# Two transformer blocks on one core: the group behind six norms multiplies x before it is normalised

## The reference, cut to what matters

```python
def rms_norm(x, w=None):                      # first block, final norm
    y = xf * lax.rsqrt(jnp.mean(jnp.square(xf), axis=-1, keepdims=True) + EPS)
...
    x = x + g1 * (mixed @ w_out[l])
    h2 = rms_norm(x) * (1.0 + sc2) + sh2
    x = x + g2 * (jnp.square(jax.nn.relu(h2 @ w_ff1[l])) @ w_ff2[l])
    return rms_norm(x, final_norm_w)

def layer_norm(x, g, b):                      # second block
    mu = jnp.mean(xf, axis=-1, keepdims=True)
    var = jnp.mean(jnp.square(xf - mu), axis=-1, keepdims=True)
    y = (xf - mu) * lax.rsqrt(var + LN_EPS)
    return (y * g.astype(jnp.float32) + b.astype(jnp.float32)).astype(x.dtype)

def swiglu(x, w_gu, w_down):
    g, u = jnp.split(x @ w_gu, 2, axis=-1)
    return (jax.nn.silu(g) * u) @ w_down
...
        x = layer_norm(DEEPNORM_ALPHA * x + 0.5 * swiglu(x, ffn_w_gu[i, 0], ffn_w_down[i, 0]), ln_g[i, 0], ln_b[i, 0])
        y = moba_attention(...) or pool_mixer(...)
        x = layer_norm(DEEPNORM_ALPHA * x + y, ln_g[i, 1], ln_b[i, 1])
        x = layer_norm(DEEPNORM_ALPHA * x + 0.5 * swiglu(x, ffn_w_gu[i, 1], ffn_w_down[i, 1]), ln_g[i, 2], ln_b[i, 2])
```

## Time and profile before

| what | value |
|---|---|
| time, median of 3 executions | 1534.44 us (1533.14 to 1536.07) |
| profiled execution, first to last instruction | 1538.2 us |
| TensorE busy | 1504.7 us (98%) |
| VectorE busy | 1085.1 us (71%) |
| ScalarE busy | 824.3 us (54%) |
| POOL busy | 184.3 us (12%) |
| mean granted TensorE clock | 0.996 |
| dummy products at the borders (L868) | 147, of 10345 TensorE products |

### The profile page before, as it was taken

One profiled execution on the slowest core, in us unless ns is written; L12 is line 12 of the kernel. 1 busy time (PEld: TensorE's weight loads), 2 busy tenths in 40 slices (PEclk: granted clock), 3 DMA queues, 4 the chain that ended last, 5 costly groups with the idle time before them and its releaser, 6 DMA issues.

```text
span 1538.2 us, 26135 instructions
## 1 busy us (share of the span) xinstructions
PE 1504.7 (98%) x10345; PEld 1389.6 (90%) x10345; DVE 1085.1 (71%) x1409; ACT 824.3 (54%) x1067; POOL 184.3 (12%) x169
## 2 busy tenths in 40 slices
PE   8999999999999999999999999999999999999997
PEld 7999998989988899888998988889988898988887
DVE  7788988787877656666576686665766659876655
ACT  5655567654555336555444555554655545565543
POOL 0120003562000010000130020001300013020001
PEclk9999999999999999999999999999999999999999
DMA  8957756645455754455544345555455553355550
GB/s 327 364 209 274 268 193 226 226 153 218 176 197 183 269 186 166 173 192 189 192 161 168 110 165 177 193 181 187 164 178 193 182 187 135 141 191 191 189 192 28
DMA packets 43397, 295.89 MB, mean 192 GB/s; under 512 B 5052, under 2 KB 7228, under 8 KB 8750
## 3 DMA queue, kind: packets, MB, share of 16 engines
q1 hardware_dynamic: 40574, 280.24, 50.2%
q0 software_dynamic: 2736, 14.41, 2.8%
HBM read 291.44 MB, written 3.19 MB: 192 GB/s over the span
## 4 chain that ended last, share of the span: by engine, by line
PE 59%; DVE 5%; ACT 1%; DMA 0%; issue 0%; ACTq 0%; DVEq 0%
PE banks L660 25%; PE banks L662 13%; PE banks L673 5%; PE banks L676 5%; PE banks L675 5%; DVE w_lo L1698 1%; DVE XS L1871 1%; PE banks L686 1%; PE banks L691 1%; PE banks L688 1%; DVE XS L1844 1%; DVE H L1879 0%; PE banks L868 0%; DVE pw L2287 0%; PE banks L1113 0%; PE banks L1116 0%
## 5 line engine op out<-in xcount | busy, mean ns | idle before, releaser
L1698 DVE TENSOR_TENSOR w_lo<-raw,w_hi 128x1024 fp32r<-128x1024 f32 x490 | 616.5, 1277 | 309.6 <-ACT w_hi L1212 304.3
L1212 ACT ACTIVATE w_hi<-raw 128x1024 fp32r<-128x1024 f32 x490 | 509.1, 1056 | 413.9 <-PE banks L662 205.7
L660 PE MATMUL banks<-H,w_hi 128*128 128x512 f32 x1504 | 528.6, 394 | 1.7 <-DVE w_lo L1698 1.7
L662 PE MATMUL banks<-H,w_lo 128*128 128x256 f32 x1504 | 425.4, 283 | 0.0
L660 PEld LDWEIGHTS banks<-H,w_hi 128*128 128x128 f32 x1504 | 282.5, 188 | 67.3 <-DVE w_lo L1698 2.3
L662 PEld LDWEIGHTS banks<-H,w_lo 128*128 128x128 f32 x1504 | 282.8, 188 | 0.0
L660 PE MATMUL banks<-HH,w_hi 128*128 128x512 f32 x480 | 168.9, 394 | 1.4 <-DVE w_lo L1698 1.4
L802 PE MATMUL banks<-H,w_lo 128*128 128x256 f32 x512 | 147.6, 288 | 2.2 <-ACT gate_a L1376 2.2
L805 PE MATMUL banks<-H,w_hi 128*128 128x256 f32 x512 | 145.6, 284 | 0.0
L804 PE MATMUL banks<-H,w_hi 128*128 128x256 f32 x512 | 145.6, 284 | 0.0
L662 PE MATMUL banks<-HH,w_lo 128*128 128x256 f32 x480 | 135.8, 283 | 0.0
(11 more groups left out here) (313 smaller groups left out, 2525.0 us busy)
## 6 DMA issues: line engine op xcount, KB each, us to landing
raw<-in_panels SPq DMA_DIRECT2D x265, 1024.0 KB, 4.8
rows<-cum_rows POOLq DMA_DIRECT2D x16, 384.0 KB, 4.7
late_w<-in_panels POOLq DMA_DIRECT2D x4, 1024.0 KB, 5.2
bias_rows<-rev POOLq DMA_DIRECT2D x1, 2048.0 KB, 8.2
XS<-in_x_t SPq DMA_DIRECT2D x4, 256.0 KB, 5.3
near<-bias_rows POOLq DMA_DIRECT2D x8, 128.0 KB, 3.2
out_t<-XS SPq DMA_DIRECT2D x4, 256.0 KB, 2.6
ws<-in_ws_t POOLq DMA_DIRECT2D x1, 512.0 KB, 10.7
```

Source lines behind the costliest of these rows:

```text
L660: pe.matmul(bank, w_hi[:, panel_slot, at:at + P], operand[:, kk, :, :].rearrange("p a t -> p (a t)"), start=starts and c == chunks[0], sto ...
L662: return pe.matmul(bank[:, 0:T], w_lo[:, panel_slot, at:at + P], operand[:, kk, 0, :], start=False, stop=stops and c == chunks[-1])
L1212: act.activation(w_hi[:, sl, w], raw[:, r, w], ACT.Copy).then_inc(panel_hi, 1)
L1698: vec.tensor_tensor(w_lo[:, sl, w], raw[:, r, w], w_hi[:, sl, w], ALU.subtract).then_inc(panel_lo, 1)
```

## The change

For six borders (`AHEAD_OF_NORM`) the first group of the next stage is computed from the unscaled x times the norm's per-channel scale, split into high and low as usual (`U_early`, `U_late`: ScalarE `unscaled_hi`, VectorE `unscaled_lo`). As the norm's mean and root belong to a token, and a token is a column of the result, they are applied when the group is evicted: (products + (-mean) x (weights times scale)) x root + (weights times bias). The two sums per output channel come from two more columns ("edges") that hold the norm's scale and bias beside the 256 tokens, so the products have 258 columns (256 behind ff2). The mean sums (`whole_stats`) stand after the first two blocks of that group, and wait for all eight blocks to be added by VectorE (`add_block` up to block 7). H is made during that group, for the second group on. The dummy products and the separate sums of these borders are gone.

```diff
+AHEAD_OF_NORM = {"out": "ff1", "ff2": "gu0", "down0": "qk", "att_out": "gu1", "down1": "gu2", "pool_out": "gu3"}
+EDGE = 2
...
+        U_early = sb("U_early", [P, BANKS, 2, T + EDGE], F32R, inv_stack)
...
 @block.tensor
+            def unscaled_group(name):
+                s, stage = INDEX[name], BEFORE_STAGE[name]
+                width = T if stage == "ff2" else T + EDGE
+                psum_free(s, 0)
+                for p in range(2):
+                    q = FIRST_PANEL[s] + p
+                    for half in range(2):
+                        pe.wait_ge(panel_lo, 2 * q + half + 1)
+                        for c in (2 * half, 2 * half + 1):
+                            k = BANKS * p + c
+                            pe.wait_ge(S["unscaled_lo"], unscaled_count(stage, k))
+                            both = unscaled(k)
+                            for b in range(BANKS):
...
+                                pe.matmul(acc, w_lo[:, q % SPLIT, at:at + P], both[:, 0, 0:width], start=k == 0, stop=False)
+                                pe.matmul(acc, w_hi[:, q % SPLIT, at:at + P], both[:, 1, 0:width], start=False, stop=False)
+                                last = pe.matmul(acc, w_hi[:, q % SPLIT, at:at + P], both[:, 0, 0:width], start=False,
+                                                 stop=k == KD - 1)
+                        last.then_inc(half_used, 1)
+                        if p == 0 and half == 0:
+                            whole_stats(stage)
+            def whole_stats(stage):
+                b, k = stat_bank(stage), NORMED.index(stage)
+                pe.wait_ge(S["norm_whole"], k + 1)
...
-            stats(2, False, "out")
-            busy_border("out")
-            stage_k8("ff1", H, norm_block(1), hi_block(1))
+            stage_k8("ff1", H, norm_block(1))
...
 @block.scalar
+            def unscaled_hi(name, m):
+                if m % BANKS == 0 and name != "ff2":
+                    act.activation(unscaled_edges(m // BANKS, 0), norm_edges(name, m // BANKS), ACT.Copy).then_inc(S["edges_hi"], 1)
+                act.activation(unscaled(m)[:, 0, 0:T], xb[:, m, :], ACT.Copy, scale=norm_scale(name)[:, m:m + 1])\
+                    .then_inc(S["unscaled_hi"], 1)
...
+                    for m in range(KD):            # first_group, ScalarE: H rounded, next panels between
+                        if m in (1, 2, 4, 6):
+                            split(q + at // 2, *raw_place(q + at // 2), halves=(at % 2,))
+                        act.wait_ge(S["norm_y"], KD * k + m + 1)
...
+            def first_biased(dest, a):             # ff1 and qk
+                def rest(s, G, next_half):
+                    act.wait_ge(S["first_scaled"], UNSCALED_ORDER.index(BEFORE_STAGE[STAGES[s][0]]) + 1)
+                    for b in range(BANKS):
+                        act.activation(dest(G)[:, b, :], dest(G)[:, b, :], ACT.Identity, bias=edges[:, b, a:a + 1])\
+                            .then_inc(S["first_kept"], 1)
+                    next_half(0)
+                    next_half(1)
...
 @block.vector
+            def last_group_unscaled(name, g, G, new_x):
+                alone = name in SUMMED_AHEAD
+                adds = {3: (5, 6)} if alone else {0: (1, 2), 1: (3,), 2: (4, 5), 3: (6,)} if name == "att_out" else \
+                    {1: (4,), 2: (5,), 3: (6,)}
+                for b in range(BANKS):
+                    bank_post(INDEX[name], g, G, b, new_x)
+                    if b == BANKS - 1:
+                        unscaled_lo(name, BANKS + b - 1)
...
+                    for m in adds.get(b, ()):
+                        add_block(name, m)
+                    if 0 < b < BANKS - 1:
+                        unscaled_lo(name, BANKS + b - 1)
+                add_block(name, KD - 1)
+                split_after(split, name, 0)
+                unscaled_lo(name, KD - 1)
...
+                def post(s, G):                    # first_group, VectorE
...
+                    split_after(split, stage_name, 1)
+                    if mean:
...
+                        for g in range(2):
+                            vec.tensor_tensor(by_group(xb)[:, g, :, :], by_group(xb)[:, g, :, :], away, ALU.add)\
+                                .then_inc(S["norm_centred"], BANKS)
+                    vec.wait_ge(S["stat_root"], n + 1)
+                    scaled(0)
+                    for m in range(KD):
+                        if m + 1 < KD:
+                            scaled(m + 1)
+                        lo(m)
+                        if m in (0, 1, 3, 5):
+                            split_half(q + at // 2, at % 2)
...
+                    products_done(s, 0)
+                    if stage_name != "ff2":
+                        vec.tensor_copy(edges[:, :, :], banks[:, BANKS * G:BANKS * G + BANKS, T:T + EDGE])\
+                            .then_inc(S["edges_kept"], 1)
+                    if mean:
...
+                        for b in range(BANKS):
+                            last = vec.scalar_tensor_tensor(first[:, b, :], st[:, 0, :], edges[:, b, 0:1],
+                                                            banks[:, BANKS * G + b, 0:T], ALU.mult, ALU.add)
+                        last.then_inc(taken, 1)
+                        vec.wait_ge(taken, FIRST_GROUP[s] + 1)
+                        vec.tensor_tensor(first, first, root, ALU.mult).then_inc(S["first_scaled"], 1)
+                    else:
+                        vec.tensor_tensor(first, group_banks(G), root, ALU.mult).then_inc(taken, 1)
...
+                    rest(s, G, lambda half: split_half(q + SPLIT, half))
...
-            layer_norm("att_out", 1)
```

More of the change, by code:

```diff
@@ L93 @@
 SUMMED_AHEAD = tuple(n for n in NORMED if n not in ("out", "att_out", "pool_out"))
+AHEAD_OF_NORM = {"out": "ff1", "ff2": "gu0", "down0": "qk", "att_out": "gu1", "down1": "gu2", "pool_out": "gu3"}
+BEFORE_STAGE = {after: stage for stage, after in AHEAD_OF_NORM.items()}
+UNSCALED_ORDER = [n for n in NORMED if n in AHEAD_OF_NORM]
+WHOLE_NORM = [n for n in NORMED if n not in AHEAD_OF_NORM]
+CENTRED = tuple(n for n in NORMED if n not in ("out", "ff2"))
+EDGE = 2
 WIDE = ("ff1", "gu0", "gu1", "gu2", "gu3")
@@ L106, with rests_kept @@
 URGENT = ("add1", "deep", "keep", "scale")
-def wide_before(stage):
-    return sum(s[2] for s in STAGES[:stage] if s[0] in WIDE)
+def rests_kept(stage, g):
+    earlier = sum(s[2] - (s[0] in BEFORE_STAGE) for s in STAGES[:stage] if s[0] in WIDE)
+    return earlier + g + (STAGES[stage][0] not in BEFORE_STAGE)
 def panels_of(stage):
@@ L204, in two_blocks @@
         mod = sb("mod", [P, 48])
+        edges = sb("edges", [P, BANKS, EDGE])
         phase = ExitStack()
@@ L447, in body @@
                         take_up(s, g, (FIRST_GROUP[s] + u) % 2)
-                groups(eng, s, body)
+                if first is None:
+                    groups(eng, s, body)
+                    return
+                first(s, FIRST_GROUP[s] % 2)
+                split(*ahead(s, 1, 1, None, 1))
+                take_up(s, 1, (FIRST_GROUP[s] + 1) % 2)
+                groups(eng, s, body, begun=1)
                 return
@@ L666, in product @@
                     if wide:
+                        if ready is not None and b == 0:
+                            ready(k + c - chunks[0] + 1)
                         return wide_product(b, c)
@@ L1549, in _ @@
             stage("out", squares_post)
[L1550 to L1551 removed]
             act.wait_ge(S["c_kept"], 1)
[L1553 removed]
+            stage("ff1", relu2_post, first_group("out", 1, ev8, mod[:, 24:32], first_biased(lambda G: ev[:, G, :, :], 0)))
             stage("ff2", squares_post)
[L1555 to L1556 removed]
             norms = [3]
@@ L1840, in take_up, with split_and_low @@
                             add_block(name, m)
+                def split_and_low(q, *place, halves=(0, 1)):
+                    (own_split or split)(q, *place, halves=halves)
+                    if q == through(INDEX[name], 0) + SPLIT:
+                        for m in range(BANKS):
+                            unscaled_lo(name, m)
+                if name in AHEAD_OF_NORM:
+                    run(vec, INDEX[name], split_and_low, take_up)
+                    return
                 run(vec, INDEX[name], own_split or (split if name in SUMMED_AHEAD else split_but_last(name)), take_up)
@@ L2192, in _ @@
             stage_x("out", gated_x(16))
-            apply_norm(1, ev8, mod[:, 32:40], mod[:, 24:32], "out")
-            stage("ff1", relu2_post)
+            stage("ff1", relu2_post, first_group("out", 1, ev8, mod[:, 24:32], first_relu2))
             def split_and_mods(q, *place, halves=(0, 1)):
```

258 lines of the change are left out of this document (217 added, 41 removed).

## The result

The kernel after takes 1522.74 us (median of 4, 1519.46 to 1525.12); the kernel before, on the same chip, 1534.62. The ratio is 0.9912 (95% interval 0.9896 to 0.9928): faster by 0.9%, 12 us by the medians and 13.5 by the ratio. The border work came out nearly as forecast. Most of the gain came from somewhere the prediction did not look.

The account below looks back on a forecast made before the run. The prediction took TensorE's chain to bound the kernel, with VectorE deciding at the changed borders. Border gains of 6.6 us, cut to 2.4 by clock falls, took the median of 1534.44 to 1532.0 us, range 1523 to 1540.

Parts of the forecast that it names:

- From the third group on the stage runs as it did: Stages behind each border: unchanged from the third group on, so borders are priced only up to that group's start.
- signs of being wrong: New products not 0.12 us apart, VectorE evicting gu2's first group well before t0 + 24, or the clock holding.
- The border sum: Six borders, clock falls included: -1.3 + 3.5 - 1.8 + 0.5 + 0.9 + 0.6 = 2.4 us gained.
- VectorE decides: Down1 to gu2: VectorE's chain sets the third group's start at about t0 + 26.2; TensorE arrives at 23.9.
- The waits inside the groups: First groups of ff1, gu1 and gu3: TensorE waits 3.9, 5 and 3.4 us for VectorE's added blocks.
- The clock: New waits in ff1, qk, gu1, gu2 and gu3: each lowers TensorE's clock and costs 1.6 us, partly covered.
- The prediction's one case: Trace before the change: a 2.17 us wait before 242.28, then granted clock 0.57, 1.6 to 1.7 us of work lost.
- 258 columns: First groups' new products: priced beside those of 256 columns, adding 0.1 us a border.
- Clock stays up: Rival, new waits: waits of this length need not lower the clock; gain 6.6 us, 1527.8 us; chance 0.20.
- TensorE is the bound: Rival, all six borders: VectorE keeps up, third group at 23.5 to 24.2; gain 30 us, 1504; chance 0.06.
- Clock low twice as long: Rival: another 1.6 us in ff1, qk and gu2, 0.9 each in gu1 and gu3; 1538.6 us; chance 0.15.
- The new products cost more: Rival, first groups: products dearer than 256 columns, each 0.01 us costing 6 us on TensorE; chance 0.11.

Follow-up runs that it names:

- edges last: The kernel after with the tile `edges` allocated last, so all other tiles lie as in the kernel before: 1533.57 us, ratio 0.9975.
- the sooner panel: The kernel after with the third group's first half panel rounded and subtracted sooner at qk and gu2: 1517.52 us, ratio 0.9873.
- sums-later run: The kernel after with the whole sums behind out, att_out and pool_out multiplied after four blocks instead of two: 1521.14 us, ratio 0.9904.
- 96 bytes: The kernel before with an unused tile of 96 bytes behind `mod`, moving H, HH and the rest: 1537.78 us, ratio 1.0006.
- 64 bytes: The kernel before with an unused tile of 64 bytes behind `mod`, moving H, HH and the rest: 1529.27 us, ratio 0.9954.

## Why the prediction was right and wrong

**The step that failed** is "From the third group on the stage runs as it did": the prediction carried the spacing of products ("dense products of 256 columns start every 0.119 us") over unchanged to the kernel after, and so put the time behind G2 at no change, without a reason. The new tile moved the operands by 32 bytes; a pair went from 0.3511 to 0.3467 us, a triple on HH from 0.3560 to 0.3520, and the stages between the borders became some 1% shorter: 9.9 of the 15.4 us between the two profiled executions. No term of the sum and no rival held that; it is why 1532.0 became 1522.7. None of the signs of being wrong that the prediction names came: the new products are 0.12 us apart, VectorE evicts the first group of gu2 by t0 + 23.4, the clock fell. All of them watch the borders. Undoing the move alone gives 1533.57.

**The border sum was right in size**: 3.0 us in the profile of after, 3.8 (1.5 to 6.1) by the run without the move, 1.2 against the kernel before moved likewise, where 2.4 was forecast. That it came so near is luck in part, as the errors on the clock cancel. In its parts:

- *VectorE decides.* In gu2 it was to reach the eviction at t0 + 21.5 and did at 21.57. VectorE's timeline there answers to the earlier trace rows:
```profile
1092.11 0.16 DVE L2165 COPY edges<-banks 128x8 f32<-128x8 f32 x1
1092.31 1.65 DVE L2170 SCALAR_TENSOR_TENSOR ev<-st,edges,banks 128x256 f32<-128x256 f32 x4
1093.99 1.23 DVE L2174 TENSOR_TENSOR ev<-ev,st 128x1024 f32<-128x1024 f32 x1
1095.14 1.22 DVE L1868 TENSOR_TENSOR w_lo<-raw,w_hi 128x1024 fp32r<-128x1024 f32 x1
```
  Edges, four of 0.40, root, half panel: the forecast order. From the eviction's start to G2 it takes 4.3 us, forecast 4.6; the root is the cheapest against its price (1.15 start to start, taken as 1.27).
- *The waits inside the groups*: 3.44, 4.55 and 3.02 us, forecast 3.9, 5 and 3.4; the sums came at t0 + 6.5, 7.6 and 6.05, forecast 6.7, 7.8 and 6.2.
- *The clock* was taken at 1.6 us a fall from one case. It fell in four places out of five. The three inside a group cost 2.3 to 2.6, qk 1.5, gu2 nothing (the wait there was 1.72 us). The errors cancel: ff1 lost 0.9 us more than forecast, gu2 gained 1.9 more. The prediction's one case was itself a matter of the execution: in the profile of the kernel after the clock held at 1.00 behind the same wait (1.98 us ahead of 240.22). So was the size: falls behind the same three waits cost 1.4 us in places (ff1 and gu3 with edges last, gu3 with the sooner panel), and at ff1 none came with the sooner panel.
- *258 columns*: 0.1199 us a product in gu2 and 0.1187 for 256 columns in gu0 (means of 93 start-to-start distances in the first groups), so 0.1 us a border, as taken.

**The rivals.** "Clock stays up" gave the nearest time, 1527.8, but not for its reason: the clock fell. "TensorE is the bound" is refuted by G2's waits on w_lo in the kernel after and the sums-later run. "Clock low twice as long" comes near in length at ff1, gu1 and gu3, and 0.8 and 0.6 us reach G2 in gu1 and gu3, where this rival had 0.9 each; but nothing was lost in gu2. "The new products cost more" is refuted by the 0.1199 us.

## What to carry to other kernels

A change that allocates anything moves what is allocated behind it; before a gain of a per cent is credited to the algorithm, time the old kernel with the same tiles moved, and the new one with them put back. In a kernel bound by TensorE, compare the spacing of untouched products first: it tells a global effect from a border effect within one view. When a wait inside a chain is taken away and the next engine's panel is only just in time, expect the wait behind it. Filling such a wait so that the clock holds gave 5 us here; shortening it gave as much at the borders in one trace and nothing that the medians show, so which is better is not settled.

## What the runs showed of the hardware

- The spacing of back-to-back products changes when the operand's tile moves against the weights' tiles: 0.3467 to 0.3533 us for the same pair, 0.340 to 0.356 for a narrow triple on H in the first stage. 32 bytes changed the whole kernel by 0.8%; moving weights and operands together changed nothing (1.0011).
- The distance alone does not fix the spacing: with 96 bytes a wide stage ran through at 0.3533 or at 0.3467 us on the same tiles, and with 64 bytes triples of one line took 0.3533 us on HH and 0.3400 on H.
- Moving only one of the two weights' distances gave no part of the gain on the wide products (395 and 396 ns, against 392 with both). The mechanism was not found.
- Falls of the clock behind waits of 3.0 to 4.6 us inside the first groups cost 1.4 to 2.6 us each; one such wait (3.44 us) had none. Behind waits of 2.0 to 2.4 us (qk with the sooner panel, ff1's G2 with the later sums) it fell in 5 of 7 cases, behind the 1.72 us in gu2 of the kernel after not.
